# Column halves at two residual sums, band products of 144 columns and moved weight splits in a 1-core three-layer fp32 kernel

## The reference, cut to what matters

```python
# layer 1: hybrid_layer (gated linear attention + sliding-window attention, conv feed-forward)
# layers 2 and 3: second_block
for layer in range(2):
    u = rmsnorm(h, g[0])
    m = mixer_fox_nsa(u, ...) if layer % 2 == 0 else mixer_pool(u, pool_w[i], pool_scale[i])
    h = h + rmsnorm(m, g[1])
    u = rmsnorm(h, g[2])
    h = h + rmsnorm((silu(u @ w_gate[layer]) * (u @ w_up[layer])) @ w_down[layer], g[3])
```

## Time and profile before

| | |
|---|---|
| median of 3 runs | 1665.63 us (1665.28 to 1665.72) |
| the profiled execution | 1666.04 us, its span 1664.3 us |
| busy, share of the span | PE 98%, PE weight loads 81%, DVE 53%, ACT 43%, POOL 10% |
| granted PE clock, mean | 0.995 of full |

### The profile page before, as it was taken

How to read it: one execution, slowest core, us unless ns; L and a number is a source line. 1 busy time by engine, 2 the same in 40 slices (tenths; PEclk the granted TensorE clock), 3 DMA queues, 4 the chain that set the end, 5 groups by cost and what they waited for, 6 DMA issues and landing times.

```text
span 1664.3 us, 22461 instructions
## 1 busy us (share of the span) xinstructions
PE 1632.6 (98%) x8132; PEld 1355.0 (81%) x8132; DVE 883.8 (53%) x1470; ACT 709.9 (43%) x1205; POOL 166.3 (10%) x249
## 2 busy tenths in 40 slices
PE   8999999999999999999899999999999999999997
PEld 7777788888888887888777888888899788888887
DVE  5644667777743356676646544443248644444233
ACT  4555454444432226677646332232236523233231
POOL 2011000000000022445402000002000200000001
PEclk9999999999999999999999999999999999999999
DMA  5211223332333242121112233233331123333331
GB/s 181 89 39 40 88 89 101 101 98 91 92 107 93 89 129 77 39 64 52 52 55 85 89 100 98 91 101 98 92 114 59 56 90 99 101 90 100 101 102 51
DMA packets 57159, 144.89 MB, mean 87 GB/s; under 512 B 14160, under 2 KB 20976, under 8 KB 57088
## 3 DMA queue, kind: packets, MB, share of 16 engines
q1 hardware_dynamic: 55680, 141.58, 27.5%
q0 software_dynamic: 688, 1.26, 0.4%
q10 hardware_dynamic: 720, 1.10, 0.2%
HBM read 138.67 MB, written 2.10 MB: 85 GB/s over the span
## 4 chain that ended last, share of the span: by engine, by line
PE 92%; ACT 3%; DVE 3%; issue 1%; DMA 1%; ACTq 0%; POOL 0%; DVEq 0%
PE ps L1970 26%; PE ps L1972 25%; PE ps L1971 25%; PE ps L2071 1%; PE ps L2070 1%; PE ps L2069 1%; PE ps L2139 1%; PE ps L2363 1%; PE ps L2378 1%; PE ps L2416 1%; PE ps L2364 1%; PE ps L2129 1%; DMA x<-xT 1%; PE ps L2535 0%; PE ps L2202 0%
## 5 line engine op out<-in xcount | busy, mean ns | idle before, releaser
L1970 PE MATMUL ps<-hhi,whi 128*128 128x512 f32 x1400 | 553.1, 395 | 3.0 <-DVE wlo L1330 2.3
L1971 PE MATMUL ps<-hlo,whi 128*128 128x512 f32 x1400 | 546.3, 390 | 0.0
L1972 PE MATMUL ps<-hhi,wlo 128*128 128x512 f32 x1400 | 546.1, 390 | 0.0
L1330 DVE TENSOR_TENSOR wlo<-raw,whi 128x1024 fp32r<-128x1024 f32 x229 | 280.5, 1225 | 451.4 <-ACT whi L818 448.6
L818 ACT ACTIVATE whi<-raw 128x1024 fp32r<-128x1024 f32 x242 | 255.9, 1057 | 518.9 <-PE ps L1972 518.7
L1970 PEld LDWEIGHTS ps<-hhi,whi 128*128 128x128 f32 x1400 | 263.4, 188 | 66.6 <-issue 8.2
L1972 PEld LDWEIGHTS ps<-hhi,wlo 128*128 128x128 f32 x1400 | 263.4, 188 | 55.7
L1971 PEld LDWEIGHTS ps<-hlo,whi 128*128 128x128 f32 x1400 | 263.7, 188 | 53.8 <-issue 1.2
L1970 PE MATMUL ps<-ahi,whi 128*128 128x512 f32 x432 | 168.0, 389 | 0.0
L1971 PE MATMUL ps<-alo,whi 128*128 128x512 f32 x432 | 168.0, 389 | 0.0
L1972 PE MATMUL ps<-ahi,wlo 128*128 128x512 f32 x432 | 168.0, 389 | 0.0
(11 more groups left out here) (358 smaller groups left out, 2022.1 us busy)
## 6 DMA issues: line engine op xcount, KB each, us to landing
raw<-w_up_b SPq DMA_DIRECT2D x88, 512.0 KB, 3.5
raw<-w_up_a SPq DMA_DIRECT2D x44, 512.0 KB, 3.4
raw<-w_in_b SPq DMA_DIRECT2D x23, 512.0 KB, 3.8
raw<-w_in_a SPq DMA_DIRECT2D x19, 512.0 KB, 3.5
raw<-w_down_b SPq DMA_DIRECT2D x16, 512.0 KB, 3.5
raw<-w_out_a SPq DMA_DIRECT2D x8, 512.0 KB, 3.5
raw<-w_down_a SPq DMA_DIRECT2D x8, 512.0 KB, 3.5
raw<-w_out_b SPq DMA_DIRECT2D x8, 512.0 KB, 3.7
```

What stands on the lines that cost most here:

```text
L1330: dve.tensor_tensor(wlow(n), raw_of(n), whigh(n).bitcast(f32), ALU.subtract).then_inc(lo_done, 1)
L1970: pe_.matmul(out, wh, hi, start=start, stop=False)
L1971: pe_.matmul(out, wh, lo, start=False, stop=False)
L1972: return pe_.matmul(out, wl, hi, start=False, stop=stop)
```

## The change

Seven edits, in order of the flow.

1. For the last row block of `out_b` and of `pool` the squares, their addition, the mean, Ln and Exp run on columns 0 to 255 and 256 to 511 one after the other. The second half's mean goes to PSUM bank 6, and its Exp waits until half 0 is scaled.
2. The first row block in `ramp` is scaled, added and given its high part in the same halves; the block counts as ready after both.
3. The split of the unit behind the three fed ones (the fourth of `up_b0` and of `up_b1`), on ACT and DVE before, is done by POOL at the start of `lower`, once the second half's squares are added.
4. In the pool layer DVE splits unit 2 before the `z_out` of groups 2 and 3 of the first half (behind them before), POOL takes unit 3 after the band matrices, DVE does unit 4 after the last squares are added.
5. Three of the four band products per row block take 144 columns, and the three of 16 columns go; ahead of them a zero product (an fp32r column of zeros, broadcast on both sides) starts the bank.
6. 11 idle products after the mean in place of 14.
7. Counters follow (`STAT_BASE`, `X_BASE`, `sq_base`), and POOL fills the new tile `zero`.

```diff
-WARM = {"x": 9, "sum": 5, "rstd": 14}
+WARM = {"x": 9, "sum": 5, "rstd": 11}
+LAST_IN_HALVES = ("out_b", "pool")
+        MS_HALF = [4, 6]
+            fill(pool.memset(zero[:, :].bitcast(f32), 0.0))
@@ POOL, lower(e)
+                n = FIRST[FED[e]] + AHEAD
+                pool.wait_ge(raw_ready[n % RAW], raw_loaded(n))
+                pool.wait_ge(unit_done, FIRST[FED[e]])
+                pool.wait_ge(sq_used, sq_base[STREAMED[e - 1]] + KD + 1)
+                pool.wait_ge(hi_done, n)
+                pool.tensor_copy(whigh(n), raw[n % RAW][:, :]).then_inc(hi_done, 1)
+                pool.wait_ge(hi_done, n + 1)
+                pool.wait_ge(lo_done, n)
+                pool.tensor_tensor(wlow(n), raw[n % RAW][:, :], whigh(n).bitcast(f32), ALU.subtract).then_inc(lo_done, 1)
@@ POOL, after the band matrices
+                n = FIRST["pool"] + 3
+                pool.wait_ge(hi_done, n + 1)
+                pool.wait_ge(lo_done, n)
+                pool.tensor_tensor(wlow(n), raw[n % RAW][:, :], whigh(n).bitcast(f32), ALU.subtract).then_inc(lo_done, 1)
@@ ACT, normalized
+                if m == KD - 1 and p in LAST_IN_HALVES:
+                    for half in HALVES:
+                        act.activation(sq[:, m % 2, half], ps[:, bank, half], ACT.Square, scale=scale).then_inc(sq_ready, 1)
@@ ACT and DVE, gemm
-                        for n in range(n0 + count + 1, n0 + count + AHEAD) if k == 0 else [n0 + count + AHEAD]:
+                        for n in range(n0 + count + 1, n0 + count + AHEAD) if k == 0 else []:
@@ ACT, statistics(e)
+                if e + 1 in RAMP:
+                    for half in range(2):
+                        done = STAT_BASE[e] + half + 1
+                        act.wait_ge(ms_ready, done)
+                        act.activation(rstd[:, HALVES[half]], ps[:, MS_HALF[half], HALVES[half]], ACT.Ln, bias=epsc[:, 0:1]
+                                       ).then_inc(rstd_ln, 1)
+                        act.wait_ge(rstd_ln, done)
+                        if half:
+                            act.wait_ge(post_done, X_BASE[e] + 1)
+                        act.activation(ps[:, BANK_RSTD, HALVES[half]], rstd[:, HALVES[half]], ACT.Exp, scale=-0.5
+                                       ).then_inc(rstd_ready, 1)
+                    return
@@ ACT, ramp(e), row block 0
+                        act.wait_ge(x_done, X_BASE[e - 1] + 1)
+                        act.activation(half_tile(hhi, 0, 0), half_tile(x, 0, 0), ACT.Copy, scale=col(GAIN[e]))
+                        act.wait_ge(x_done, X_BASE[e - 1] + 2)
+                        act.activation(half_tile(hhi, 0, 1), half_tile(x, 0, 1), ACT.Copy, scale=col(GAIN[e])
+                                       ).then_inc(h_hi, 1)
@@ ACT, pool_layer
-                    if m in (0, 2):
-                        split_hi(FIRST[p] + 4 + (m == 2), 0)
+                    if m == 0:
+                        split_hi(FIRST[p] + 4, 0)
@@ DVE, summed(p, m)
+                if m == KD - 1 and p in LAST_IN_HALVES:
+                    dve.wait_ge(sq_used, sq_base[p] + m)
+                    for half in range(2):
+                        cols = HALVES[half]
+                        dve.wait_ge(sq_ready, sq_base[p] + m + half + 1)
+                        dve.tensor_tensor(sumsq[:, cols], sumsq[:, cols], sq[:, m % 2, cols], ALU.add).then_inc(sq_used, 1)
+                    return
@@ DVE, handover, behind half_lower(KD - 1, 1)
+                split_lo(FIRST["pool"] + 2, 0)
@@ DVE, ramp(e), ahead of the loop over row blocks 1 to 7
+                for half in range(2):
+                    cols = HALVES[half]
+                    out = ps[:, BANKS_T[0], cols]
+                    dve.wait_ge(rstd_ready, STAT_BASE[e] + half + 1)
+                    dve.scalar_tensor_tensor(out=out, in0=half_tile(mt, 0, half), scalar=gain, in1=ps[:, BANK_RSTD, cols],
+                                             op0=ALU.mult, op1=ALU.mult).then_inc(post_done, 1)
+                    dve.wait_ge(post_done, base + half + 1)
+                    dve.tensor_tensor(half_tile(x, 0, half), half_tile(x, 0, half), out, ALU.add).then_inc(x_done, 1)
@@ DVE, pool_layer
-                split_lo(FIRST[p] + 2, 0)
...
-                split_lo(FIRST[p] + 3, 0)
...
-                    if m == 2:
-                        split_lo(FIRST[p] + 4, 0)
-                split_lo(FIRST[p] + 5, 0)
+                dve.wait_ge(lo_done, FIRST[p] + 4)
+                split_lo(FIRST[p] + 4, 0)
@@ PE, statistics(e), behind keep_clock(e, WARM["sum"])
+                        for half in range(2):
+                            cols = HALVES[half]
+                            pe_.wait_ge(sq_used, sq_base[STREAMED[e]] + KD + half)
+                            pe_.matmul(ps[:, MS_HALF[half], cols], ones[:, :], sumsq[:, cols], start=True, stop=True
+                                       ).then_inc(ms_ready, 1)
+                        keep_clock(e, WARM["rstd"])
+                        return
@@ PE, pool_layer
+                    pe_.matmul(ps[:, MEAN_BANK[m], :], zero[:, 0:1].broadcast_to([P, P]), zero[:, 0:1].broadcast_to([P, S]),
+                               start=True, stop=False)
                     for b in range(NB):
-                        c = b * P
-                        last = pe_.matmul(ps[:, MEAN_BANK[m], c:c + P], zt[:, b, m * P:m * P + P],
-                                          band[:, 2 * g + (b == 0), 0:P], start=b == 0, stop=False)
-                    for b in range(1, NB):
-                        c = b * P
-                        last = pe_.matmul(ps[:, MEAN_BANK[m], c:c + MAXW], zt[:, b - 1, m * P:m * P + P],
-                                          band[:, 2 * g, P:P + MAXW], start=False, stop=b == NB - 1)
+                        c, w = b * P, P + MAXW if b < NB - 1 else P
+                        last = pe_.matmul(ps[:, MEAN_BANK[m], c:c + w], zt[:, b, m * P:m * P + P],
+                                          band[:, 2 * g + (b == 0), 0:w], start=False, stop=b == NB - 1)
```

More of the change, by code:

```diff
@@ L151, in build @@
         invc = sb("invc", [P, MAXW])
+        zero = sb("zero", [P, 32], f32r)
         ffn = ExitStack()
@@ L264, in build @@
         sq_ready, sq_used = sem("sq_ready"), sem("sq_used")
-        sq_base = {"out_a": 0, "down_a": 8, "out_b": 16, "down_b0": 24, "pool": 34, "down_b1": 42}
+        sq_base = {"out_a": 0, "down_a": 8, "out_b": 16, "down_b0": 25, "pool": 35, "down_b1": 44}
         zeroed = sem("zeroed")
@@ L1018, in statistics @@
             def statistics(e):
-                act.wait_ge(ms_ready, e + 1)
+                if e + 1 in RAMP:
[10 more added lines that the diff above has]
+                    return
+                act.wait_ge(ms_ready, STAT_BASE[e] + 1)
                 act.activation(rstd[:, :], ps[:, BANK_MS, :], ACT.Ln, bias=epsc[:, 0:1]).then_inc(rstd_ln, 1)
-                act.wait_ge(rstd_ln, e + 1)
-                act.activation(ps[:, BANK_RSTD, :] if e in (3, 7, 9) else rstd[:, :], rstd[:, :], ACT.Exp, scale=-0.5
+                act.wait_ge(rstd_ln, STAT_BASE[e] + 1)
+                act.activation(rstd[:, :], rstd[:, :], ACT.Exp, scale=-0.5
                                ).then_inc(rstd_ready, 1)
@@ L1029, in ramp @@
                 for m in range(KD):
-                    act.wait_ge(x_done, X_BASE[e - 1] + m + 1)
-                    act.activation(tile(hhi, m), tile(x, m), ACT.Copy, scale=col(GAIN[e], m)).then_inc(h_hi, 1)
+                    if m:
+                        act.wait_ge(x_done, X_BASE[e - 1] + m + 2)
+                        act.activation(tile(hhi, m), tile(x, m), ACT.Copy, scale=col(GAIN[e], m)).then_inc(h_hi, 1)
+                    else:
+                        act.wait_ge(x_done, X_BASE[e - 1] + 1)
[3 more added lines that the diff above has]
+                                       ).then_inc(h_hi, 1)
                     if m >= 2:
@@ L1611, in ramp @@
                 base = X_BASE[e]
-                for m in range(KD):
+                gain = gscale[:, 0:1] if e == 7 else col(GAIN[e])
+                for half in range(2):
[6 more added lines that the diff above has]
+                    dve.tensor_tensor(half_tile(x, 0, half), half_tile(x, 0, half), out, ALU.add).then_inc(x_done, 1)
+                for m in range(1, KD):
                     out = ps[:, BANKS_T[m % 2], :]
                     if m >= 2:
-                        dve.wait_ge(x_done, base + m - 1)
+                        dve.wait_ge(x_done, base + m)
                     dve.scalar_tensor_tensor(out=out, in0=tile(mt, m),
@@ L1633, in last_post @@
             def last_post(half):
-                dve.wait_ge(rstd_ready, LAST + half + 1)
+                dve.wait_ge(rstd_ready, STAT_BASE[LAST] + half + 1)
                 dve.wait_ge(evac[ENDING], END_ROWS[0] + 2 * half + 2)
```

34 lines of the change are left out of this document (18 added, 16 removed).

## The result

The changed kernel takes **1671.08 us** (median of 8 runs, 1670.41 to 1672.03), the kernel before, on the same chip, 1665.68 (8 runs, 1664.97 to 1665.87). The ratio is 1.0034 [1.0023, 1.0045]: slower by 5.4 us, where 1661.8 was forecast. The profiled execution took 1671.58 us, its span is 1669.9 and its mean granted clock 0.995, as before.

The account below looks back on a forecast made before the run. PE was taken as the bound, carrying 92% of the chain that ended last. Gains of 1.18 and 1.18 at the residual sums and 1.42 net at the band products sum to 3.78 us, giving 1661.8; range 1660.6 to 1664.2.

Parts of the forecast that it names:

- One more POOL memset: At the kernel's start: delays the constants a little, but the first product waits for x; cost 0, bounds 0 and 0.2.
- The sum of the edited places: Both residual sums and the band products together: 1.18 + 1.18 + 1.42 = 3.78 us gained.
- the joins: The two residual sums, last row block in column halves: square to first high product 5.12 and 5.28 us, gain 1.18 each.
- POOL's copy: In the weight split moved to POOL at both residual sums: taken at 1.5 us, bounds 0.77 and 2.40, hidden, cost 0.
- The group: Pool layer's band products: 1.28 us per group with zero product 0.23, so 0.28 less, times eight 2.24 us.
- The later start: Band products' first group waits for DVE's split of unit 2, now ahead of its last token groups: loss 0.82 us.
- DVE keeps up: During the band groups: DVE, with two splits fewer in its way, keeps pace at 1.28 us per group.
- A: Rival, band groups: 144-column pass dearer (0.150) or ACT sets the pace; gain 2.3 to 3.1, 1662.9 us; chance 0.15.
- B: Rival, residual sums: POOL and DVE collide, half 0 scaled at 3.8, not 2.7; 1662.9 or 1662.7 us; chance 0.08.
- C: Rival, band groups: zero product dear, change turns to loss at 0.70 us; at 0.86, 1666.9 us; chance 0.05.
- D: Rival, residual sums: halves do nothing, as filler or ACT's queue hold the first products; 1664.2 us; chance 0.04.
- E: Rival, band products: their start isn't delayed, or the 144 columns are free; 1661.0 us; chance 0.08.

Follow-up runs that it names:

- before_band: The kernel before with the new band products alone, zeros in an unused column of an existing tile: 1665.69 us, ratio 1.0001.
- band_and_splits2: The kernel before with the new band products and the moved splits around them, no halves at the sums, no new tile: 1663.91 us, ratio 0.9989.
- before_pad64: The kernel before with an unused 64-byte tile at the place of the change's new tile: 1668.11 us, ratio 1.0015.
- map_three: Separate kernel of products alone in the kernel's order and high-low distances, each operand at eight start offsets in 32-byte steps: 402.42 us, one execution.
- split_behind: The changed kernel without its new tile, DVE's split of unit 2 back behind its first-half z_out: 1661.41 us, ratio 0.9977.

## Why the prediction was wrong

**The step that failed** is the last sentence before the sum: "One more POOL memset at the start delays the constants by a little ... Cost 0, bounds 0 and 0.2." I priced the instruction that fills the new tile and not the tile. The runs showed 9.9 us for it on the changed kernel (1671.08 to 1661.19) and 9.7 on the kernel before (1675.32 to 1665.62, with no instruction added). No rival had it, and the slower side had 0.03.

**The sum of the edited places** held: 3.78 us forecast, 4.16 by the traces, 4.43 by the medians. That it is so close is partly luck, as the joins gave 0.32 less than forecast and the groups 0.86 more. Its terms:

- *The joins*, 1.18 each: 1.04 and 1.00. The chain is the ending's, as foreseen. From the earlier trace rows it was to be 5.12 us and took 5.29.
- *POOL's copy*, taken at 1.5 between 0.77 and 2.40: 1.04 alone (first sum). At the second sum it took 1.82 and ended at 1292.08, 0.91 after DVE's split had; I had it wait until that split's end. PE's high products never waited for POOL; block 0's low part (895.88 on) was in time.
- *The group*, 1.28: it was 1.175. The zero product took 0.29 (1279.03 to 1279.32), not 0.23, and the eight passes 0.88, not 1.05. The starts one by one show why: a pass of 144 columns is followed after 0.1225 us, one of 128 after 0.109 to 0.112, and the next zero product starts 0.031 after the last pass. The 0.97 of the earlier trace rows holds an interval of 0.19 behind the first pass of the group; the other seven are 0.112. So 0.121 was no price of a pass but a mean with that interval in it, and 16 more columns cost 0.010 to 0.013.
- *The later start*, 0.82: it was 0.90 (3.01 us from the token-sum product at 1276.02 to the first group, 2.11 before).
- *DVE keeps up*: right, but I booked the moved splits as a loss of 0.82 beside the groups' 2.24. `before_band` and `band_and_splits2` show that the gain hangs on them: without them the shorter groups are worth -0.08 us, with them 2.12.

**The rivals.** A didn't come: the pass of 144 columns takes 0.1225, not 0.150. B didn't: half 0 was scaled at 2.82 after the square, behind its own Exp. C: the zero product is 0.29, far from the 0.70 at which it turns. D didn't. E didn't: the start is delayed and the 144 columns aren't free; its time of 1661.0 is near the 1661.19 without the tile for another reason, the cheaper passes. Apart from the tile, the forecast of 1661.8 was right in its mechanism and wrong in the size of these terms.

## What to carry to other kernels

A tile is a change of its own: whatever is allocated behind it moves, and a dense stream of products can gain or lose 3% by the distance of its operands. When an edit adds, drops or resizes a tile, first compare the mean duration of products that the edit doesn't touch; if they moved, pad the tile so that the rest keeps its place modulo 256 bytes. And where work is taken from the bounding engine, look at the next queue (here DVE's splits) before booking the gain: it was worth nothing until that queue was shortened too.

## What the hardware showed

- An fp32r product of 512 columns in the kernel's order follows the last after 0.2267 us when its stationary and moving operand start at the same byte modulo 256, 0.2289 with 64 bytes between, 0.2333 with 128. In the ramps, where the stationary operand is the one 64 bytes further on, it was 0.2333. Products of 256 columns with the same tiles went the other way: `ahi` with `hlo` 0.1199 us apart before, 0.1186 after the change and 0.1167 in `before_pad64`. So the distance that is best for one shape need not be for another. The Trainium skill (SBUF — State Buffer, SBUF: two separate sides) says that on the engine side PE never waits on anyone. No run here shows PE held by another engine's traffic, but `map_three` shows it slower by its own two operands, with the other engines still. What in the chip does that is open.
- A wait of 1.87 us and one of 0.33 on PE were followed by 3 us at the lower clock (0.50 of full), in which the mean, on the path, took 2.00 us for 1.12.
- `gscale`, a DVE operation on 8 columns with two inputs, took 0.38 us beside POOL's split (changed kernel, POOL until 1279.82) and 0.16 without it (`split_behind`): a short DVE operation, too, pays for the other engine's long one.
